# One core, two layers of a transformer block: attention values kept per head pair, one bias table, evenly cut loads, output weights split earlier

## What is computed

```python
GRID_W, NA_HEADS, NA_HEAD_DIM, NA_KH, NA_KW = 64, 8, 64, 8, 16
def neighbourhood_attention(q, k, v, rpb):
    ...
    row_idx = jnp.clip(r - kh // 2, 0, rows - kh)[:, None] + jnp.arange(kh)[None, :]
    ...
    s = jnp.einsum('bhrcd,bhrjkd->bhrcjk', qg, kg).astype(jnp.float32) + bias[None]
    s = jnp.where(col_mask[:, None, :], s, -jnp.inf)
    p = jax.nn.softmax(s.reshape(B, NA_HEADS, rows, GRID_W, kh * GRID_W), axis=-1).reshape(s.shape)
    o = jnp.einsum('bhrcjk,bhrjkd->bhrcd', p, vg)
...
    na_out = neighbourhood_attention(na_q, na_k, na_v, rpb) * jax.nn.silu(na_z)
...
    return jnp.concatenate([na_out, ml_out], axis=-1) @ w_out
...
        h_res = h_res + gate[:, None, :] * y
```

## Time and profile before

| | |
|---|---|
| median of 3 executions | 2044.43 us (2041.75 to 2045.49) |
| the profiled execution | 2044.65 us, its span 2042.8 us, so 1.85 us lie outside the span |
| PE busy | 94% of the span |
| DVE, ACT, POOL busy | 49%, 31%, 26% |
| attention, first scores to last value product | 1504.72 us to about 1770.2 us |

### The profile page before, as it was taken

The page is one execution under the profiler, slowest core; times in us unless marked ns, Lnnn a source line. Parts: engine busy times, 40 slices in busy tenths (PEclk is TensorE's granted clock), DMA queues, the critical chain, the costliest instruction groups (busy, mean ns, idle before and its releaser), DMA issues. The chain is left out here.

```text
span 2042.8 us, 26377 instructions
## 1 busy us (share of the span) xinstructions
PE 1919.5 (94%) x9913; PEld 1567.7 (77%) x9913; DVE 1004.2 (49%) x2227; ACT 632.8 (31%) x1316; POOL 532.4 (26%) x807
## 2 busy tenths in 40 slices
PE   6999999989999999999998999999999767699998
PEld 5888878768887788888884878888877545488887
DVE  6564565564565332117772121232147556666675
ACT  5421211132334332002221012211146445555552
POOL 3122323211222221100100002222135435534442
PEclk9999999989999999999998999999999878899999
DMA  5233323344575744212120135655577764646773
GB/s 170 79 104 94 90 75 114 116 140 143 185 199 190 243 162 147 72 63 87 68 78 23 64 95 172 217 185 165 193 212 225 171 206 151 199 161 231 243 238 109
DMA packets 248922, 300.31 MB, mean 147 GB/s; under 512 B 40534, under 2 KB 182390, under 8 KB 246204
## 3 DMA queue, kind: packets, MB, share of 16 engines
q1 hardware_dynamic: 223916, 221.02, 35.9%
q0 software_dynamic: 22576, 73.42, 10.1%
q10 hardware_dynamic: 2304, 4.20, 0.5%
HBM read 199.89 MB, written 99.15 MB: 146 GB/s over the span
## 5 line engine op out<-in xcount | busy, mean ns | idle before, releaser
L145 PE MATMUL banks<-hT,wu 128*128 128x512 f32 x512 | 201.8, 394 | 1.5 <-DVE hT L217 1.5
L147 PE MATMUL banks<-hT,wu 128*128 128x512 f32 x512 | 200.0, 391 | 0.0
L146 PE MATMUL banks<-hT,wu 128*128 128x512 f32 x512 | 199.7, 390 | 0.0
L145 PE MATMUL banks<-iT,wua 128*128 128x512 f32 x384 | 150.8, 393 | 2.4 <-DVE iT L1190 2.4
L145 PE MATMUL banks<-iT,wub 128*128 128x512 f32 x384 | 152.0, 396 | 1.0 <-DVE wub L1190 1.0
L145 PE MATMUL banks<-wub,iT 128*128 128x512 f32 x384 | 150.5, 392 | 0.0
L147 PE MATMUL banks<-iT,wub 128*128 128x512 f32 x384 | 150.2, 391 | 0.0
L146 PE MATMUL banks<-iT,wub 128*128 128x512 f32 x384 | 150.0, 391 | 0.0
L147 PE MATMUL banks<-iT,wua 128*128 128x512 f32 x384 | 149.5, 389 | 0.0
L146 PE MATMUL banks<-wub,iT 128*128 128x512 f32 x384 | 149.5, 389 | 0.0
L146 PE MATMUL banks<-iT,wua 128*128 128x512 f32 x384 | 149.5, 389 | 0.0
(11 more groups left out here) (276 smaller groups left out, 4184.1 us busy)
## 6 DMA issues: line engine op xcount, KB each, us to landing
iraw<-in_w_in SPq DMA_DIRECT2D x36, 512.0 KB, 4.5
wa<-in_w_ada SPq DMA_DIRECT2D x48, 256.0 KB
v<-V SPq DMA_DIRECT2D x48, 240.0 KB, 4.7
raw<-in_pool_in_w SPq DMA_DIRECT2D x16, 512.0 KB, 4.4
yT<-sg POOLq DMA_DIRECT2D x32, 256.0 KB, 3.0
oraw<-yT SPq DMA_DIRECT2D x32, 256.0 KB, 4.2
xr<-in_x SPq DMA_DIRECT2D x16, 512.0 KB, 3.7
h<-h POOLq DMA_DIRECT2D x16, 512.0 KB, 3.4
```

Of the source, the lines that this page charges most:

```text
L145: e.matmul(ps, lh, rh, start=first, stop=False)
L146: e.matmul(ps, lh, rl, start=False, stop=False)
L147: return e.matmul(ps, ll, rh, start=False, stop=last)
```

## The change

It has these parts:

- `GatedWeights` (new): the 16 pieces of `w_out` are loaded, scaled on POOL and split on ACT and DVE beside tiles 3 to 10 of `FirstOut`, two for each tile, and both halves are stored to HBM (`wg`). The tail only loads them back (512 KB each, two for each of 8 parts) at the pairs of the new `Tail.due`. The same 16 multiplications, 16 copies and 16 subtractions leave the attention.
- Values: `nv` is stored as `VM` (the first 128 of the 160 keys of each block of 4 grid rows) and `VE` (the other 32). `VM` of a head pair is loaded once for all its pairs; for each pair only the 64 or 96 rows of `VE` are loaded. The turn on PE becomes, for each head, one 128x128 transpose per block and then one matmul with 32 columns of probabilities per block.
- One bias table of 12 rows for each head pair in place of three (1200 columns become 480), and a copy `mid` of it on POOL, into which the masks are written; `top` and `bot` read 8 rows of the table without a mask, so they have 320 scores for each query.
- Loads for the next head pair are cut into pieces of 256 or 512 KB.
- Scores are negated in the DVE instruction (scale -0.125 and a minimum), and ACT's exponential takes scale -1: the two DVE negations for each pair go.
- The split of the gates' weights moves to unit 18 of `Proj`.
- Places in SBUF of the tail's buffers, and the pairs at which its first loads stand, move.

```diff
--- before.py
+++ after.py
...
+    def jobs(self, m):
+        return range(2 * m - 6, 2 * m - 4) if 3 <= m < 3 + KT else ()
...
+        if m == 3:
+            w.wait_ge(*self.out.mixer.mixed.ge(32))
+            for i in range(3):
+                w.wait_ge(*self.out.mixer.sg_st[i].ge(11 - i // 2))
+            e.dma_start(self.row[:], k.mod[0, 2 * D:3 * D].partition_broadcast(P)).then_inc(*self.row_in.inc())
+        for j in self.jobs(m):
+            if j >= 2:
+                w.wait_ge(*self.low.ge(j - 1))
+            src = k.io["w_out_2"][0][j // 2 * P:(j // 2 + 1) * P, j % 2 * W:(j % 2 + 1) * W]
+            e.dma_start(self.raw[j % 2][:], src).then_inc(*self.raw_in[j % 2].inc())
...
+            e.activation(self.hi[j % 2][:], self.raw[j % 2][:], ACT.Copy).then_inc(*self.high.inc())
...
+            e.tensor_tensor(self.lo[j % 2][:], self.raw[j % 2][:], self.hi[j % 2][:].bitcast(F32), ALU.subtract).then_inc(*self.low.inc())
...
+    def store(self, e, w, j):
+        dst = [self.k.wg[p, j // 2, :, j % 2 * W:(j % 2 + 1) * W] for p in range(2)]
+        w.wait_ge(*self.high.ge(j + 1))
+        e.dma_start(dst[0], self.hi[j % 2][:].bitcast(F32)).then_inc(*self.st[j % 2].inc())
...
+        e.dma_start(dst[1], self.lo[j % 2][:].bitcast(F32)).then_inc(*self.st[j % 2].inc())
+    def pool(self, e, w, m):
+        for j in self.jobs(m - 1):
+            self.store(e, w, j)
+        for j in self.jobs(m):
+            w.wait_ge(*self.raw_in[j % 2].ge(j // 2 + 1))
+            w.wait_ge(*self.row_in.ge(1))
+            e.tensor_tensor(self.raw[j % 2][:], self.raw[j % 2][:], self.row[:, j % 2 * W:(j % 2 + 1) * W], ALU.mult).then_inc(*self.gated.inc())
...
-            if name == "gates" and tb == 0:
+            if n == 3 * NU:
                 jobs.append(("gates",))
...
+                    r4 = 2 * (m % 2) + y
+                    for a, c0 in enumerate((0, 24)):
+                        b, nc = 64 * y + c0, 40 if r4 < 3 else 8
+                        src = self.st[i % 2][b:b + nc, :].rearrange("c (hp d) -> c hp d", hp=4)
+                        e.dma_start(k.VM[:, 40 * r4:40 * r4 + nc, m // 2, a, :].rearrange("hp c d -> c hp d"), src).then_inc(*self.v_st[i % 2].inc())
+                        if r4 == 3:
+                            e.dma_start(k.VE[a, m // 2], self.st[i % 2][b + 8:b + 40, :]).then_inc(*self.v_st[i % 2].inc())
...
-KINDS = {"top": (480, 9, 7), "mid": (0, 12, 3), "bot": (840, 9, 2)}
+KINDS = {"top": (8, 4), "mid": (12, 0), "bot": (8, 0)}
...
+        self.jobs = ([("t", ri) for ri in range(4)] + [("q", x, y) for y in range(4) for x in range(4)] + [("v", x) for x in range(2)]
+                     + [("z", x) for x in range(2)])
         self.due = {p: [] for p in range(self.NP + 3)}
         for hp in range(3):
-            jobs = [("q", x) for x in range(4)] + [("t", x, ri) for x in range(3) for ri in range(4)] + [("z",)]
-            for n, j in enumerate(jobs):
-                self.due[16 * hp + (3 if hp else 0) + n * 10 // 17].append((hp + 1, j))
+            for n, j in enumerate(self.jobs):
+                self.due[16 * hp + (3 if hp else 0) + n * 10 // len(self.jobs)].append((hp + 1, j))
...
+        elif j[0] == "v":
+            if hp >= 2:
+                w.wait_ge(*self.o_full.ge(16 * (hp - 1)))
+            g = slice(4 * j[1], 4 * j[1] + 4)
+            e.dma_start(self.vm[b][:, g], k.VM[hp, :, g]).then_inc(*self.vm_in[b].inc())
...
+            r, y0 = slice(32 * j[1], 32 * j[1] + 32), 4 - j[1]
             for a in range(2):
-                e.dma_start(self.tabs[b][32 * ri:32 * ri + 32, :, a, off:off + nk * 40],
-                            k.Z[a, 2 * hp:2 * hp + 2, :, y0 * 40:(y0 + nk) * 40].rearrange("h c y -> c h y")).then_inc(*self.tab_in[b][x].inc())
+                e.dma_start(self.tab[b][r, :, a, :],
+                            k.Z[a, 2 * hp:2 * hp + 2, :, y0 * 40:(y0 + 12) * 40].rearrange("h c y -> c h y")).then_inc(*self.tab_in[b].inc())
...
-                    w.wait_ge(*self.negated.ge(n + 1))
+                    w.wait_ge(*self.s_out.ge(n + 1))
                     if n >= 8:
                         w.wait_ge(*self.pt_full.ge(n - 7))
-                    e.activation(self.pr[n % 8][:, 0:N], self.sr[n % 4][:, 0:N], ACT.Exp, bias=self.st[:, n, 1:2],
-                                 accum_out=self.st[:, n, 2:3]).then_inc(*self.raised.inc())
+                    e.activation(self.pr[n % 8][:, 0:N], self.sr[n % 4][:, 0:N], ACT.Exp, bias=self.st[:, n, 0:1], scale=-1.0,
+                                 accum_out=self.st[:, n, 1:2]).then_inc(*self.raised.inc())
...
-                    e.tensor_tensor_reduce(out=self.sr[n % 4][:, 0:N], in0=self.pS[n % 4][:, 0:N], in1=self.tabs[hp % 2][:, hh, a, off:off + N],
-                                           scale=0.125, scalar=-3.0e38, op0=ALU.add, op1=ALU.max,
+                    e.tensor_tensor_reduce(out=self.sr[n % 4][:, 0:N], in0=self.pS[n % 4][:, 0:N], in1=tab[:, hh, a, 40 * u0:40 * u0 + N],
+                                           scale=-0.125, scalar=3.0e38, op0=ALU.add, op1=ALU.min,
                                            accum_out=self.st[:, n, 0:1]).then_inc(*self.s_out.inc())
-                    w.wait_ge(*self.s_out.last())
-                    e.tensor_scalar(self.st[:, n, 1:2], self.st[:, n, 0:1], -1.0, None, ALU.mult).then_inc(*self.negated.inc())
...
+        if part < 2:
+            w.wait_ge(*self.tab_in[hp % 2].ge(8 * (hp // 2 + 1)))
+            if hp >= 2:
+                w.wait_ge(*self.s_out.ge(32 * (hp - 1)))
+            e.tensor_copy(mid[:, part], tab[:, part]).then_inc(*self.blocked.inc())
+            return
...
-            if p % 16 == 14 and p // 16 < 3:
-                for kind in self.kinds:
-                    self.block(e, w, p // 16 + 1, kind)
+            if 9 <= p % 16 < 13 and p // 16 < 3:
+                self.block(e, w, p // 16 + 1, p % 16 - 9)
...
-                nj = self.window(q)[1] // 3
+                a, nb = self.pairs[q][2], self.blocks(q)
                 for x in range(2):
                     n = 2 * q + x
+                    probs = self.pr[n % 8]
                     w.wait_ge(*self.scaled.ge(n + 1))
                     if q >= 1:
                         w.wait_ge(*(self.pt_act if x else self.pt_dve).ge(q))
-                    for j in range(nj):
-                        t = e.transpose(self.pT[x][0:120, j * P:(j + 1) * P], self.pr[n % 8][:, j * 120:(j + 1) * 120], self.ident[:])
+                    for j in range(nb):
+                        e.transpose(self.pT[x][:, j * P:(j + 1) * P], probs[:, 160 * j:160 * j + P], self.ident[:])
+                    for j in range(nb):
+                        t = e.matmul(self.pT[x][32 * j:32 * j + 32, nb * P:(nb + 1) * P], probs[:, 160 * j + P:160 * (j + 1)], self.ident[:],
+                                     start=True, stop=True)
...
-                for j in range(nj):
+                for j in range(nb + 1):
                     for hh in range(2):
-                        t = e.matmul(self.pO[64 * hh:64 * hh + 64, 0:P], self.vr[q % 4][:, j, 64 * hh:64 * hh + 64],
-                                     self.ptr[(2 * q + hh) % 4][:, j * P:(j + 1) * P], start=(j == 0), stop=(j == nj - 1))
+                        d = slice(64 * hh, 64 * hh + 64)
+                        r = slice(0, P) if j < nb else slice(0, 32 * nb)
+                        v = self.vm[hp % 2][:, g0 + j, a, d] if j < nb else self.vr[q % 4][r, d]
+                        t = e.matmul(self.pO[d, 0:P], v, self.ptr[(2 * q + hh) % 4][r, j * P:(j + 1) * P], start=(j == 0), stop=(j == nb))
...
-        self.due = {34: 0, 37: 1, 40: 2, 43: 3} | {50 + x: 4 + x for x in range(12)}
+        self.due = {18: (0,), 36: (1,), 50: (2,), 54: (3,), 57: (4,), 60: (5,), 62: (6,), 64: (7,)}
...
+        for x in self.due.get(p, ()):
+            if x >= 2:
+                w.wait_ge(*att.s_full.ge(48))
+                w.wait_ge(*att.s_out.ge(96))
+                w.wait_ge(*att.o_full.ge(48))
+            for y in range(2):
+                e.dma_start(self.ws[x][:, y].bitcast(F32), k.wg[y, x]).then_inc(*self.w_in.inc())
...
-            w.wait_ge(*self.gated_w.ge(j + 1))
-            if j >= 4:
-                w.wait_ge(*self.att.s_full.ge(48))
-                w.wait_ge(*self.att.s_out.ge(96))
-            e.activation(self.ws[j // 2][:, 0, j % 2 * W:(j % 2 + 1) * W], self.raw[j % 2][:], ACT.Copy).then_inc(*self.w_hi.inc())
...
-            e.tensor_tensor(self.ws[j // 2][:, 1, sl], self.raw[j % 2][:], self.ws[j // 2][:, 0, sl].bitcast(F32), ALU.subtract).then_inc(*self.w_lo.inc())
...
-            w.wait_ge(*self.w_in[j % 2].ge(j // 2 + 1))
-            w.wait_ge(*self.row_in.ge(2))
-            r, sl = self.raw[j % 2], slice(j % 2 * W, (j % 2 + 1) * W)
-            e.tensor_tensor(r[:], r[:], self.A[:, sl], ALU.mult).then_inc(*self.gated_w.inc())
```

(39 more changed lines are left out.)

215 lines of the change are left out of this document (112 added, 103 removed).

## The result

The changed kernel takes **1992.15 us** (median of 4 executions, 1988.89 to 1993.57) against 2044.92 us (2041.75 to 2045.49) for the kernel before, a ratio of 0.9743 (95% interval 0.9726 to 0.976). That is 52.8 us less; the forecast was 31.7 less, with 1985 to 2038 us as its range. The direction was right and the time is in the range, but the gain is two thirds larger than the sum said.

What follows compares the result with a forecast made beforehand. PE was taken to bound the kernel, elsewhere whatever PE waits for. From 2044.65 us, -12.2 - 74 + 49.5 + 2 + 2 + 1 = -31.7 gave 2012.9, forecast as 2013 us, range 1985 to 2038.

Steps and rivals of the forecast that it cites:

- The gates: At the gates, PE's 9.97 us wait for `wg` and the slow matmuls behind it go: -12.2 us.
- The weights leave the attention: In the attention, POOL's lateness from `w_out` work and late values go; 82 us lost, 8 left: -74 us.
- loads or POOL stay late: Rival in the attention: 25 of the 82 lost us remain, from uncovered copies or late pieces; 2030 us, chance 0.15.
- What PE gets: PE's turns in the attention: more shape changes at 0.14 us, narrow matmuls at 0.11 us each; +49.5 us.
- three at once: Rival for PE's turns: a head's three 32-column matmuls run together, 0.22 us and not 0.33; 2002 us, chance 0.10.
- changes are cheap: Rival for PE's turns: transposes and narrow matmuls run into each other, 26 us less; 1987 us, chance 0.14.
- The edges: Attention's start +2 us (POOL's copies), its end +2 (loads near the tail's first loads), layer one +1.

Runs made afterwards that it cites:

- the third kernel: Kernel before with only the gates' split moved to unit 18 and the w_out pieces split beside layer one; values, turns and tables as before: 1994.38 us, ratio 0.9752.
- the run with one group: Changed kernel with all narrow matmuls written into rows 0 to 31, one column group in place of three: 2038.63 us, ratio 0.9975 to the kernel before.
- the grouped version: Changed kernel with the transposes of both heads first, then the narrow matmuls of both: 1974.79 us, ratio 0.9661 to the kernel before.

## Why the prediction was right, and where its sum was off

**The gates** (-12.2): right. The wait is gone, the first matmul starts 10.9 us earlier (1092.86 to 1081.96), and the matmuls behind it run at full clock at once. Alone, it measured 10.9 us by the span.

**The weights leave the attention** (-74 of 82 lost us, 81.5 before rounding): the mechanism was right, the size too small by 7, and the reason given was incomplete. From 1506.91 us to the last product's end at 1718.72 pass 211.8 us. PE's own groups there, by their spacings, are 47.7 (scores), 99.1 (turns), 63.7 (products) and 1 of the tail, 211.5: no more than the wait of 0.5 us on DVE is lost, and not 8. POOL's copies are covered: behind the start no wait on POOL is left, with 1.0 us for a copy and not 1.3. But the text gave nearly all of the 82 us to the weights alone, with a side remark on two late values. Moved alone, they gave 39, and with the gates 28.7 us of waits stayed. With POOL late, the loads of values for each pair and of three tables had time that they lost when POOL was not. The rival "loads or POOL stay late" described that case. It failed for the whole change, which also makes the loads smaller and fewer: from 1540 to 1700 us the share of the DMA engines is 0.56 at 169 GB/s after, and 0.83 at 229 in the kernel with the two moves alone. Whether it was the bytes or the number of issues (24 for the tables of a head pair and now 8) is open: the shares speak for the bytes, SyncE's timeline of the third kernel for the tables' issues, and no run took out either alone.

**What PE gets** (+49.5): it got 40.2 (211.8 less the wait of 0.5, against 171.1 us before for the same pairs). Two sizes were off. The narrow matmuls of a head of a long pair take 0.35 us and not 0.47, 2 x 0.12 x 48 = 11.5 less: this was the rival "three at once", and it came true in full. The step that failed is the one that took 0.11 for a narrow matmul "from the value products", whose 64 columns leave room for two, while 32 leave room for more; the argument that each is two records which must follow each other did not count. By its chance of 0.10 the text held this for unlikely. The Trainium skill ("TensorEngine Tiling (Array Packing)", Tiling Modes) has 128x32 tiles that run independently, and the run with one group agrees. In short pairs the products take 0.95 and not 0.81, 15 x 0.14 = 2.1 more, since the last one has 64 rows; "the number of value products doesn't change" was true and not enough.

The price of a change of shape, 0.14 us from one matmul of one column in the earlier trace rows, held wherever the runs could show it: in the transposes (0.48 = 3 x 0.11 + 0.14), in one group (0.77 and 0.56, 0.21 apart for one matmul), with it in the narrow matmuls (0.35 = 0.21 + 0.14), in the grouped version (two changes less, 0.27), and in the product of 64 rows. The rival "changes are cheap" is out, although the time came within some 5 us of its 1987, nearer than to the 2002 of the rival that came true: the rows for the transposes decide that, not the time. That the whole gain passed 2002 is due to the lost time and the tail.

**The edges.** The start of the attention costs 2.3 us more (12.8 to 15.1 from the first scores to the steady part), near the forecast (2), and partly by luck: the two copies took 1.9 us and not 2.6, so PE is idle 1.4 us longer (5.0 us for 3.6), and the other 0.9 us are more work of PE's own, which the text had not put there. The end was forecast 2 us slower and is 1.8 faster. The wait of 2.5 us on `ib`, which the kernel before has there too, is gone. In the kernel with the two moves alone PE has 5 us of waits on `ib` and "issue" there and its tail takes 5.8 us longer, so the earlier first loads of the tail, costed in the prediction as a risk of later ones, are worth some 5, as an estimate: no run moved them alone. In layer one +1 was forecast; PE's busy time there fell by 0.14 us in 100, and the DMA share rose to 0.76 and not to 0.86. POOL got 34 us more there and not at most 20, of which 13 are the issues of the stores, and its idle time covered it. The first scores start 13.0 us earlier where these terms give 11.2.

The sum of the differences: narrow matmuls and products -9.3, lost time -7.0, the tail -3.8, the rest -1.4, which are the 21.5 us between -31.7 and -53.2. The rest is less than the same point differs by between two profiles (the last section).

## What to carry to other kernels

When a wait of the bounding engine is removed, look at what else ran in its shadow: here moving the weights gave some 39 us of the 81 that were lost, the others went only with smaller and fewer loads, and reordering the loads moved the wait without shortening it. What the smaller loads won was paid for in PE's own work. Price short matmuls by groups and not one by one: here three that lie side by side in different column groups cost together what one costs (0.21 us), and each change of shape 0.14 us more, so groups of one shape belong together. A change of several parts can equal two of its parts and still be the base of a better version: grouping the turns gave 17 us that exist only with the new turns.

## What the runs showed of the hardware that was not expected

- Three float32 matmuls of 128 rows by 32 columns in three column groups took 0.21 us together, 0.63 in one group; each is two records, and the two records of one did not keep the others from overlapping.
- A matmul over 64 rows behind one over 128 cost 0.14 us, one over 96 rows nothing.
- Copies of 128 to 192 KB from HBM to HBM for each pair, in the queue that also loads SBUF, made the issue behind them take 1.3 to 5.0 us and not 0.3, at a DMA share of 0.56: such a queue can hold up its issuer while the DMA engines are half idle.
- Between profiles of kernels that are equal up to there, the same point of the program (the gates) lay between 1078.62 and 1083.62 us: spans of two single profiles tell apart no less than about 5 us here.
